# A four-layer hybrid decoder step on one core: old index pages split over two load times, two pages per transpose, index products in both row halves

## What is computed

```python
ik_past = cache_ik[page_table].reshape(DB, past, IDX_DIM)      # 8 x 1024 x 64
s = einsum('bqhd,bsd->bqhs', iq, ik) * (IDX_DIM ** -0.5)       # 4 heads
score = einsum('bqh,bqhs->bqs', iw * (IDX_HEADS ** -0.5), relu(s))
score = where(k_pos <= q_pos, score, -inf)
_, idx = top_k(score, topk)
```

## Time and profile before

| | |
|---|---|
| time, median of 3 runs | 1341.63 us (1340.28 to 1348.27) |
| the profiled execution | 1342.47 us, of which 1340.7 us is the span of the profile |
| PE busy | 1240.4 us, 93% of the span |
| DVE, ACT, POOL busy | 582.3, 568.5 and 372.0 us |
| chain that ended last | 73% PE, 6% ACT, 6% SP's queue, 4% DVE, 3% DMA, 3% POOL |
| PE's granted clock | 0.948 of full speed on average |

### The profile page before, as it was taken

One profiled execution on the slowest core, in us unless ns is written; L12 is line 12 of the kernel. 1 busy time (PEld: TensorE's weight loads), 2 busy tenths in 40 slices (PEclk: granted clock), 3 DMA queues, 4 the chain that ended last, 5 costly groups with the idle time before them and its releaser, 6 DMA issues.

```text
span 1340.7 us, 24586 instructions
## 1 busy us (share of the span) xinstructions
PE 1240.4 (93%) x9709; PEld 1056.8 (79%) x9709; DVE 582.3 (43%) x1175; ACT 568.5 (42%) x1097; POOL 372.0 (28%) x322
## 2 busy tenths in 40 slices
PE   7999999799569999999997999999979999999797
PEld 5679887797313899889896456999979878987696
DVE  4242345546001999920002553559444334245542
ACT  6442477433031233454454444422253244256733
POOL 5244221233020333113220002435414334321220
PEclk8899999899855999999998999999999999999898
DMA  7224234131150134666666996222222223315301
GB/s 200 64 63 142 80 110 163 35 99 34 30 190 0 52 109 148 206 214 228 221 220 240 397 336 203 64 84 79 91 85 66 95 63 110 95 61 176 110 2 67
DMA packets 132714, 168.70 MB, mean 126 GB/s; under 512 B 25448, under 2 KB 98408, under 8 KB 132591
## 3 DMA queue, kind: packets, MB, share of 16 engines
q1 hardware_dynamic: 120537, 152.54, 35.3%
q10 hardware_dynamic: 12062, 14.59, 3.1%
HBM read 150.65 MB, written 16.81 MB: 125 GB/s over the span
## 4 chain that ended last, share of the span: by engine, by line
PE 73%; ACT 6%; SPq 6%; DVE 4%; issue 4%; DMA 3%; POOL 3%; ACTq 1%; DVEq 0%
PE psum L662 18%; PE psum L664 18%; PE psum L663 18%; PE psum L1095 3%; POOL w_lo L626 3%; PE psum L1036 2%; PE psum L1199 2%; SPq L513 2%; SPq L514 2%; DMA raw<-in_cache_k_dram 1%; ACT w_hi L1287 1%; PE psum L1169 1%; PE psum L912 1%; PE psum L1150 1%; PE psum L1111 1%
## 5 line engine op out<-in xcount | busy, mean ns | idle before, releaser
L626 POOL TENSOR_TENSOR w_lo<-raw,w_hi 128x512 fp32r<-128x512 f32 (+2 forms) x267 | 350.2, 1343 | 872.8 <-ACT w_hi L1287 872.8
L662 PE MATMUL psum<-h_hi,w_hi 128*128 128x272 f32 (+1 forms) x1616 | 474.7, 294 | 21.8 <-DVE h_lo L2096 15.7
L664 PE MATMUL psum<-h_hi,w_lo 128*128 128x272 f32 (+1 forms) x1616 | 470.4, 291 | 0.0
L663 PE MATMUL psum<-h_lo,w_hi 128*128 128x272 f32 (+1 forms) x1616 | 468.1, 290 | 0.0
L662 PEld LDWEIGHTS psum<-h_hi,w_hi 128*128 128x128 f32 (+1 forms) x1616 | 303.7, 188 | 35.1 <-issue 28.1
L663 PEld LDWEIGHTS psum<-h_lo,w_hi 128*128 128x128 f32 (+1 forms) x1616 | 304.2, 188 | 1.3
L664 PEld LDWEIGHTS psum<-h_hi,w_lo 128*128 128x128 f32 (+1 forms) x1616 | 303.3, 188 | 0.9
L1287 ACT ACTIVATE w_hi<-raw 128x1024 fp32r<-128x1024 f32 (+2 forms) x137 | 133.5, 1023 | 184.6 <-PE psum L664 139.2
L662 PE MATMUL psum<-w_hi,h_hi 128*128 128x512 f32 (+3 forms) x400 | 144.7, 362 | 0.4 <-ACT idx_relu L1566 0.4
L663 PE MATMUL psum<-w_lo,h_hi 128*128 128x512 f32 (+3 forms) x400 | 141.4, 354 | 0.0
L664 PE MATMUL psum<-w_hi,h_lo 128*128 128x512 f32 (+3 forms) x400 | 141.1, 353 | 0.0
(11 more groups left out here) (301 smaller groups left out, 1553.1 us busy)
## 6 DMA issues: line engine op xcount, KB each, us to landing
raw<-in_cache_k_dram SPq DMA_DIRECT2D x128, 256.0 KB, 3.1
raw<-in_gla_w_in_dram SPq DMA_DIRECT2D x23, 1024.0 KB, 5.3
spare<-in_cache_v_dram SPq DMA_DIRECT2D x36, 512.0 KB, 6.3
raw<-in_dsa_w_in_dram SPq DMA_DIRECT2D x17, 1024.0 KB, 6.2
raw<-in_cache_v_dram SPq DMA_DIRECT2D x28, 512.0 KB, 5.9
gla_s_in<-in_state_gla_dram SPq DMA_DIRECT2D x16, 512.0 KB, 7.9
raw<-in_gla_w_out_dram SPq DMA_DIRECT2D x8, 1024.0 KB, 6.9
out_dram<-gla_s_in ACTq DMA_DIRECT2D x16, 512.0 KB, 4.1
```

The costliest lines, as they stand in the source:

```text
L626: pool.tensor_tensor(pair_view(w_lo, key)[:, k], raw_view(key)[:, k], pair_view(w_hi, key)[:, k].bitcast(F32), ALU.subtract)\
L662: pe.matmul(out, lh, rh, start=start, stop=False)
L663: pe.matmul(out, lh, rl, start=False, stop=False)
L664: return pe.matmul(out, ll, rh, start=False, stop=stop)
```

## The change

Three things are changed together.

1. The 64 pages are two tiles of 32: `idx_early` (sequences 0 to 3) and `idx_late` (4 to 7). `idx_early` has a place of its own in the region of the index tiles. SP now issues the early pages in three groups: 16 after the load of the last output weights of layer 0, 8 after the load of `ikw`, 8 after that of `iq`. The first group waits until layer 0's inputs of the output product are written (`h_lo`) and its state is stored (`stores_gla`). The 32 late pages stand where all 64 stood.
2. `turn_old` handles a sequence at once: each of the four transposes takes two pages, 128 x 128, so that the keys of the even page lie in partitions 0 to 63 and those of the odd page in 64 to 127. `ik_old` and `iq_seq` have 128 partitions, with the queries in both halves; DVE copies the lower half of `iq_seq` to the upper one. There are 8 steps in place of 16, each with eight products: for each head one with the lower 64 rows into bank 0 and one with the upper 64 rows into bank 1.
3. Both ReLUs come after the last step, and write their 128-key blocks alternately, so that the keys are in order again; the first product with `w_sel` waits for both.

```diff
-        idx_pages = at("idx_pages", [P, DB * NPAGE, ID], F32, qk_at)
+        idx_late = at("idx_late", [P, DB // 2 * NPAGE, ID], F32, qk_at)
...
+            def old_keys(half, first, end):
+
+                for col in range(first, end):
+                    at_col = half * (4 * NPAGE) + col
+                    r = sp.value_load(ptab[0:1, at_col:at_col + 1], min_val=0, max_val=cache_k.shape[1] - 1)
+                    sp.dma_start(idx_pages[half][:, col, :], cache_idx_k[0, bass.ds(r, 1)].rearrange("a p n -> (a p) n"))\
+                        .then_inc(*sig(f"idx_pages{half}", n=16))
...
-                if key == (L, "k", 0, 1) and KINDS[L] == 1:
-
-                    sp.wait_ge(*on("proj", ("item", (L - 1, "out", 3))))
-                    for col in range(DB * NPAGE):
-                        r = sp.value_load(ptab[0:1, col:col + 1], min_val=0, max_val=cache_k.shape[1] - 1)
-                        sp.dma_start(idx_pages[:, col, :], cache_idx_k[0, bass.ds(r, 1)].rearrange("a p n -> (a p) n"))\
-                            .then_inc(*sig(f"idx_pages{col // (4 * NPAGE)}", n=16))
+                if key == (0, "out", 3):
+                    sp.wait_ge(*on("h_lo", (0, "out"), SMP, 1))
+                    sp.wait_ge(*on("stores_gla", 0))
+                    old_keys(0, 0, 16)
+                if key == (1, "ikw"):
+                    old_keys(0, 16, 24)
+                if key == (1, "iq"):
+                    old_keys(0, 24, 32)
+                if key == (1, "k", 0, 1):
+
+                    sp.wait_ge(*on("proj", ("item", (0, "out", 3))))
+                    old_keys(1, 0, 32)
...
-                    for pg in range(4):
-                        mm = pe.transpose(psum[0:ID, kb, pg * P:(pg + 1) * P], idx_pages[:, b * NPAGE + 4 * c + pg, :],
-                                          ident[:])
+                    for x in range(NPAGE // 2):
+                        o = b % 4 * NPAGE + 2 * x
+                        mm = pe.transpose(psum[:, kb, x * P:(x + 1) * P],
+                                          idx_pages[b // 4][:, o:o + 2, :].rearrange("p c n -> p (c n)"), ident[:])
...
                     for h in range(IH):
-                        mm = pe.matmul(psum[h * NS:(h + 1) * NS, c, :], iq_seq[:, h, b, :], ik_old[:, b % 2, :],
-                                       start=b == 0, stop=b == DB - 1)
+                        for odd in range(2):
+                            r = slice(odd * ID, (odd + 1) * ID)
+                            mm = pe.matmul(psum[h * NS:(h + 1) * NS, odd, :], iq_seq[r, h, b, :], ik_old[r, b % 2, :],
+                                           start=b == 0, stop=b == DB - 1)
...
+                dve.wait_ge(*on("iq_seq", L, 0))
+                dve.tensor_copy(iq_seq[ID:P], iq_seq[0:ID]).then_inc(*sig("iq_seq", L))
```

More of the change, by code:

```diff
@@ L1016, in dsa, with turn_old @@
                 pe.wait_ge(*on("iq_seq", L))
[L1017 to L1019 removed]
+                def turn_old(b):
                     if b % 4 == 0:
                         pe.wait_ge(*on(f"idx_pages{b // 4}", "all"))
[L1022 to L1026 removed]
@@ L1032, in dsa @@
+                    mm.then_inc(*sig("idx_turned", L, b))
+                turn_old(0)
+                for b in range(DB):
+                    if b + 1 < DB:
+                        turn_old(b + 1)
                     if b == 0:
-                        claim(c, ("idx_s", L, c), ("idx_relu_s", L, c))
-                    pe.wait_ge(*on("ik_old", L, c, b))
+                        for odd in range(2):
+                            claim(odd, ("idx_s", L, odd), ("idx_relu_s", L, odd))
+                    pe.wait_ge(*on("ik_old", L, b))
@@ L1035, in dsa @@
                     for h in range(IH):
-                        mm = pe.matmul(psum[h * NS:(h + 1) * NS, c, :], iq_seq[:, h, b, :], ik_old[:, b % 2, :],
-                                       start=b == 0, stop=b == DB - 1)
-                    mm.then_inc(*sig("idx_s", L, c, b, also=(((L, c),) if b == DB - 1 else ())))
+                        for odd in range(2):
+                            r = slice(odd * ID, (odd + 1) * ID)
+                            mm = pe.matmul(psum[h * NS:(h + 1) * NS, odd, :], iq_seq[r, h, b, :], ik_old[r, b % 2, :],
+                                           start=b == 0, stop=b == DB - 1)
@@ L1039, in dsa @@
+                    mm.then_inc(*sig("idx_s", L, "old", b))
                 claim(2, ("idx_s", L, 2), ("idx_relu_s", L, 2))
@@ L1584, in dsa @@
                 after_item(L, "k", 0, 1)
-                for c in range(2):
-                    for b in range(DB):
-                        act.wait_ge(*on("idx_turned", L, c, b))
-                        if (c, b) >= (0, 2):
-                            q = c * DB + b - 2
-                            act.wait_ge(*on("idx_s", L, q // DB, q % DB))
-                        copy(ik_old[:, b % 2, :], psum[0:ID, bank_of("oldT", L, c, b), :])\
-                            .then_inc(*sig("ik_old", L, c, b))
-                    act.wait_ge(*on("idx_s", L, c))
-                    act.activation(relu_s[:, c * BLK:(c + 1) * BLK], psum[:, c, :], ACT.Relu, scale=sc)\
-                        .then_inc(*sig("idx_relu_s", L, c))
+                for b in range(DB):
+                    act.wait_ge(*on("idx_turned", L, b))
+                    if b >= 2:
+                        act.wait_ge(*on("idx_s", L, "old", b - 2))
+                    copy(ik_old[:, b % 2, :], psum[:, bank_of("oldT", L, b), :]).then_inc(*sig("ik_old", L, b))
+                act.wait_ge(*on("idx_s", L, "old", DB - 1))
+                for odd in range(2):
+                    act.activation(relu_s[:, 0:PAST].rearrange("p (g c t) -> p c g t", c=2, t=PAGE)[:, odd],
+                                   psum[:, odd, :].rearrange("p (g t) -> p g t", g=NPAGE // 2), ACT.Relu, scale=sc)\
+                        .then_inc(*sig("idx_relu_s", L, odd))
                 act.wait_ge(*on("idx_s", L, 2))
```

21 lines of the change are left out of this document (8 added, 13 removed).

## The result

The changed kernel took 1298.07 us (median of 4 runs, 1285.93 to 1304.64), beside 1344.95 us for the kernel before in the same comparison: a ratio of 0.964 with a 95% interval of 0.955 to 0.973. That is 46.9 us less, where I had forecast 57.6 off the median of 1341.63; the time lies 0.07 us above the upper end of the range, and outside the 1280 to 1288 that the forecast itself had with 66%. In two later comparisons the same kernel took 1296.17 and 1293.01 us, 49.0 and 53.2 us less than the kernel before beside it.

A forecast was written before the change was run, and what follows sets the result against it. PE was taken to bound the kernel, idle behind SP's page loads, then at half clock on old keys. Savings of 26.0 + 31.9 + 0.2 = 58.1 us gave 1284 us; range 1279 to 1298, some 90%, with 1280 to 1288 at 66%.

The forecast's parts named there:

- The wait: Before the old keys: 32 pages leave the queue ahead of `q`, 0's load; first product at 357.3, not 383.27, 26.0 us saved.
- The early pages delayed nobody: SP's early loads leave `ikw`, `iq` and `k`, 0 about 7 us of room or more, so cost nothing; delay rival 5%.
- 1.7 us to spare: At ACT's split of `q`, 0: the load lands at 337.7, PE frees the place at 339.4, so the load holds nothing up.
- The stage: Old keys' transposes and products, 8 steps: 12.1 us with 3.4 us at half clock, 31.9 us less than before.
- Eight products for the price of four: Old keys: row halves overlap, so eight products take 0.93 us at full clock, 1.86 at half; taking turns was an 11% rival.
- The clock in the stage: PE's clock falls at the stage's start, returns under 128-row products after 3.4 us at half, which lose 1.7 us.
- The tail: Last old-key product to `q`, 0: two ReLUs about 1.3 us, products 1.7, copy and semaphores 0.9; sum 3.9, 0.2 saved.
- The DVE copy of `iq_seq`: DVE's added 64 x 1024 copy: estimated 0.53 us, counted at nothing, at most 1.5 us if it meets POOL's work.
- The gap from `k`, 0's end to `q`, 0's start: On PE, the wait plus the old-key work and its end: 19.8 us instead of 77.9.
- So all that follows moves up as a whole.: Behind `q`, 0's start at 373.3: nothing waits, top-k and loads keep their distance, so no time is lost there.
- the rival in which the clock stays at half through the stage: Old keys: clock never comes back, 20.8 us and 5.6 after it, 47.6 us saved, 1294 us; chance 14%.

The follow-up runs named there:

- Part 1 alone: The kernel before with only the early page loads and split tile, keeping old one-page transposes, 64-row products and ReLUs: 1318.65 us, ratio 0.979 to the kernel before.
- part 2 alone: The kernel before with two-page transposes and products in both row halves, all 64 pages loaded at the old place: 1321.08 us, ratio 0.982 to the kernel before.
- the split moved: The changed kernel with ACT's split of the first half of `k`, 1 moved behind the stage's ReLUs: 1285.9 us, ratio 0.957 to the kernel before.

## Why the prediction was right, and where it was not

**The wait (26.0 us): right.** SP's 32 late pages took 34.61 us for 35.4. From the end of `k`, 0 to the first product it is 3.8 us in each of three profiles of the changed kernel, where it was 29.8: 26.0 us less. The first product was to come at 357.3; it came at 364.27, 357.59 and 354.94, since `k`, 0 itself ends at 360.45, 353.8 and 351.1. Part 1 alone gave 26.5 us in time. The early pages delayed nobody: the splits of `ikw`, `iq` and `k`, 0 lie at 284.87, 296.95 and 304.34 (285.19, 297.27, 304.66). ACT's wait for the load of `q`, 0 is gone in each profile: what its split waits for is PE. The "1.7 us to spare" was of the right order. In the last profile, where PE is not late, the load lands at 334.47 and the split starts at 337.31, released by PE: 2.8 us.

**The stage (43.95 to 12.1 us): right in its mechanism, 1.0 us too small.** From 364.27 to the end of the eighth group, 377.4, it is 13.1, and 13.2 in the two other profiles. "Eight products for the price of four" holds: 1.96 us at half clock. But a step at full clock has a pitch of 1.61 us (369.02 to 370.63), not 0.93 + 0.5 = 1.43: at full clock a group is 1.02 and the four transposes 0.59. Halving the durations of half clock was a little too good: at full clock already a group of four is 0.99 from its start to the next row's (353.75 to 354.74 in the run of part 1 alone), not 0.93. The Trainium skill, "TensorEngine Tiling (Array Packing)", Tiling Modes, lets eight 64 x 32 tiles load and multiply in parallel. The trace agrees: eight products take 1.02 us at full clock, four took 0.99.

**The clock in the stage: right.** "I take 3.4 us at half": it was 3.4 us in each of the three profiles of the changed kernel (in the last one from 355 to 359), and none where the pause ahead of the stage was 1.00 us in place of 2.94.

**The tail (4.11 to 3.9): right in size.** From the last group's end to `q`, 0 it is 3.9 us. The two ReLUs, which no row of before showed in a row, took 1.08 us for the 1.3 that I had taken. The DVE copy of `iq_seq` took 0.69 us, more than the estimate of 0.53, and held up nobody; it was counted at nothing, and that was right.

**The gap from `k`, 0's end to `q`, 0's start was to be 19.8 us; it is 20.9** in all three profiles. `q`, 0 was to start at 373.3. It started at 381.34, 374.68 and 372.04, 50.0, 56.7 and 59.3 us earlier than in the earlier trace rows.

**The step that failed is "So all that follows moves up as a whole."** From the start of `q`, 0 to the end of the span the kernel before takes 909.4 us (1340.7 less 431.33), and 912.3 in its second profile. The changed kernel takes 921.6, 921.9 and 921.5. So 9 to 12 us of the 58 are lost again behind the stage, in all three. The prediction had this term at nothing, because loads and top-k keep their distance from `q`, 0; it left out that PE's clock behind the stage need not stay the same. PE is busy at half clock there for 22.0 and 30.0 us before and for 41.8, 41.8 and 41.9 after. What half clock costs is half of that; without it the rest is 898.4 and 897.4 us before and 900.7, 901.0 and 900.5 after. So 6 to 10 us of the loss are half clock, and 2 to 4 us are not. Two places hold most of it. The stretches are cut at pauses of PE that each profile has:

| from ... to | before, two profiles | changed, three |
|---|---|---|
| `q`, 0 to the wait for `dsa_ast` | 295.2, 294.6 | 298.9, 299.3, 298.6 |
| to the wait for `smp_p` | 98.2, 99.9 | 100.5, 100.5, 100.5 |
| to the wait for `pool_rows` | 162.4, 163.6 | 163.8, 163.8, 163.9 |
| to the end of the span | 353.7, 354.3 | 358.4, 358.3, 358.5 |

In the first, PE transposes cached pages and waits for their loads. In sum that is 7.8 to 8.5 us against 5.9 and 5.4, and in each of the three the clock falls for 3.4 us behind one of the waits. In the last profile a block takes 3.54 us in place of 1.97:

```profile
526.32 3.54 PE L1113 MATMUL psum<-ident,raw 128*128 128x128 f32 x16 [2.68 <-DMA raw<-in_cache_k_dram]
...
533.65 1.97 PE L1113 MATMUL psum<-ident,raw 128*128 128x128 f32 x16
```

SP starts these loads as long after `q`, 0 as before (61.7 to 61.8 us in all five). The longest wait before was 1.41 us in one profile and 1.69 in the other, with no fall; with 1.89, 2.53 and 2.68 us there was one. That is no threshold: in the run of part 2 alone a wait of 1.88 us has none behind it. In the last stretch it is the 16-row gate products of layer 3: PE is busy at half clock for 3.4 us in both profiles of the kernel before and for 10.2 in all three of the changed one, which costs half of the difference, 3.4 us. With 128 rows the last stretch is 352.7 to 353.7 us, as short as before. So much is settled: the lost time is half clock and a few late loads. It is not settled why the same gate products fell for longer in every profile of the changed kernel, and for only 3.4 us in that of one near relative (the split moved). The cause of that stays open; the wait of 0.52 us ahead of them is the same.

Part of the distance between 1298 and 1284 is the start that it was counted from: the kernel before has medians of 1344.95 to 1346.19 us in the later comparisons, and the profiled execution, 1342.47, which all steps are made against, was one of its faster ones. And the forecast took no account of a fall of the clock ahead of the stage, such as that at 317 to 335; that one costs about 7 us, where it occurs. For the profiled execution of 1304.64 us the steps close: `q`, 0 comes 8.0 us later than forecast, and 12.2 us are lost behind it, together the 20.2 us between 1304.64 and 1284.4.

The measured time is also near the 1294 of the rival in which the clock stays at half through the stage. The profile shows that this is chance: the stage did what the forecast said, and the missing time lies elsewhere.

## What to carry to other kernels

Read a stage's granted clock beside the number of rows that its products use. Work that fills few of the array's rows ran at half clock here while the engine counted as busy. Pairing two such inputs in both row halves brought the clock back; so did padding with zeros at the gate products, which removes no work at all. When a change moves much, forecast a range for the parts behind it too: product groups with few rows, and pauses like those of 1.9 to 2.9 us here, are places where the clock may fall in one execution and not in another, here 6 to 10 us in 1300. To compare profiles, take from each span half of the time that PE was busy at half clock: that gives 1294.3 and 1292.7 us for the kernel before and 1260.6, 1262.4 and 1261.8 for the changed one, so by this estimate 30 to 34 us come from the work and the waiting that the change removes, and the rest of the 47 to 53 us from the clock. Time times mean clock is a rougher measure. It was within 5 us in the 14 runs of the changed kernel, which lie 19 us apart, but ten runs of the kernel before, 7 us apart in time, go from 1264 to 1275, since its clock is also at half while PE stands idle.

## What the runs showed of the hardware

- Half clock with hardly any idle time: 44 us of a stage of 64-row products in four bands (part 1 alone), PE busy in all but 0.3 us, at 0.50. The Trainium skill, "TensorE: Matmul & The Clock Gate", Part 1: The HAM clock gate, ties the low level to idle stretches; here rows with PE fully busy show it as well, so the measurement decides.
- With rows of zeros added the clock stayed up: under the 16-row gate products it fell in each of ten profiles, under the same products over 128 rows in none of three, and that was worth 8 to 13 us (1285.19 against 1293.01 to 1298.07, from different comparisons).
- A second row half costs 0.03 us a group at either clock: 1.96 against 1.93 us at half, and 1.09 against 1.06 at full, for twice the products.
- A small indexed load costs SP about 1.1 us of its queue: 70.84 / 64 is 1.107 before, 17.50 / 16 and 34.61 / 32 are 1.09 and 1.08 after, early and late. The early groups of eight took less, 0.99 and 1.04 us a page (7.95 and 8.34 us).
